# Masks and relative bias of attention: added by VectorE in PSUM, fused with the row maximum, in place of matmuls

## The chip, the cores and the metric

The kernel runs on one core of one Trainium2 chip. The metric is the device time of one execution in microseconds. Before the change it is 3609.16 us in the median of three runs (3609.14 to 3613.13).

## What is computed

A sequence of T = 512 tokens of width 1024 goes through two blocks of two layers each. The first block mixes with RWKV-7 heads beside four causal attention heads ("MOBA"; at this length plain causal attention) in layer 0 and with dilated attention in layer 1. The second block mixes, in both of its layers, with differential attention, retention and a short convolution, gated. MLPs follow each mixer. What matters here are the three kinds of attention:

```python
# MOBA: 4 heads of width 128, causal
p = softmax(q @ k.T * 128**-0.5  where key <= query)

# dilated: 8 heads; three query groups share keys and values; one softmax over all three
#   group q0: keys at distance 0..128; q1: every 4th key; q2: every 16th key (all causal)
wts = softmax(stack(lses));  o = sum(wts[g] * outs[g])

# differential: 4 heads, two maps of width 64 each, bias by distance from a table of 32 buckets
s = einsum('bhmqd,bhmkd->bhmqk', qb, kh) + bias[None, :, None]
s = where(dist >= 0, s, neg)
p = softmax(s);  a = p[:, :, 0] - lam * p[:, :, 1];  o = a @ v
```

## The kernel before

**Layout.** Activations lie transposed: channels on the 128 partitions (P), the 512 tokens (T) in the free dimension, as tiles of 128x512 f32. All weights stream from HBM in units of up to 128x1024 through a ring of three slots. ScalarE copies a unit to its high half (`split_hi`, L326), VectorE subtracts to get the low half (`split_lo`, L334), and TensorE does three matmuls of 512 columns for each 128x128 tile (`product`, L352 to L354). The halves are made three units ahead.

**Order of work.** A stage is a list of (work, tick) pairs; `run` walks the same list once for each engine, so each engine issues its instructions in that order and waits on semaphores. `behind` puts followers between the ticks of a lead. In the attention stages the lead is `project` (one weight unit for each tick, 8x3 matmuls, then for most tiles a rope on VectorE, L584 to L588), and attention follows with one unit for each tick. Stages end with all engines meeting; each stage begins with what SyncE (SP) is given in `loads`, and then SP refills the weight ring.

**Attention.** `attention` (L767) does one unit for each head and each block i of 128 queries; i runs over 0 to 3, so MOBA has 16 units, the dilated stage 32, and each differential layer 16. G is the number of score maps of a unit: 1, 3 and 2. In a tick u TensorE transposes the probabilities of the unit before (L812), computes for each map the scores of unit u against (i+1) key blocks (L822, f32, which the hardware takes as two passes; the dilated group q0 only against the last two blocks), and then adds masks and biases: for each key block one more matmul into the same PSUM region (L824). A mask is `ident` times a 128x128 bf16 mask tile (`k.m`), a bias is a 128x128 f32 piece of a Toeplitz tile times `flip`, the matrix that reverses the order. Then it multiplies the values with the probabilities of the unit before (L833) once ScalarE has copied the transposed probabilities (L847) and VectorE has copied the output of the unit two before (L866).

VectorE waits for all scores and adds of the unit, takes the maximum of each map (L873), then either scales both (L876, differential) or takes the maximum over the maps and scales it (L879, L880). ScalarE does exp with the row sum (L854). VectorE combines the maps and normalises (L884 to L888 or L893 to L896).

**Adds by stage.** MOBA has one mask for each unit (16). A dilated head has 27 (two maps with i+1 blocks and one with at most 2, over i = 0 to 3), eight heads 216. A differential head has 20 biases and 8 masks; four heads and two layers make 160 biases and 64 masks.

**Bias by distance.** In `prologue` (L452) TensorE and ScalarE make a row of 640 values for each of the four heads, on four partitions. SP stores it to DRAM (`bias_dram`, L475), waits for the store (L476) and for the loads (L477), and then the stage ends. At the head of each differential stage `load_bias` reads four Toeplitz tiles of 128x512 from it. `head_norms` prepares queries and keys of that stage; its GpSimd part zeroes four half tiles.

Of the kernel before, what the change touches and what calls it, by code (L numbers as in the profile page):

```python
# [72 lines left out]
SECOND = [("cos2", T), ("sin2", T), ("decay", 4 * T), ("mean128", P), ("flip", P)]  # L73
CONST_PARTS = [layout(part) for part in (COMMON, FIRST, SECOND)]
CONSTS, CONST_W = layout(COMMON + FIRST + SECOND)
MASKS = ["ident", "causal", "band", "four", "fourcausal", "sixteen", "sixteencausal"]
# [3 lines left out]
def constants():  # L80
    c = np.zeros((P, CONST_W), np.float32)

    def put(name, value):
        at, width = CONSTS[name]
        c[:, at:at + width] = value
# [28 lines left out]
    put("flip", a + b == P - 1)  # L114
# [11 lines left out]
    masks = {"ident": (d == 0) * 1.0, "causal": np.where(d >= 0, 0, NEG), "band": np.where(d <= 0, 0, NEG),  # L126
             "four": np.where(d % 4 == 0, 0, NEG), "fourcausal": np.where((d % 4 == 0) & (d >= 0), 0, NEG),
             "sixteen": np.where(d % 16 == 0, 0, NEG), "sixteencausal": np.where((d % 16 == 0) & (d >= 0), 0, NEG)}
    m = np.concatenate([masks[k] for k in MASKS], 1).astype(np.float32)

    dist = np.maximum(np.arange(T + P) - (P - 1), 0)
# [74 lines left out]
class Core:  # L206


    def __init__(self, nc, ctx, wts):
# [8 lines left out]
        self.mask = ctx.enter_context(nc.sbuf_tensor("mask", [P, len(MASKS) * P], BF16))  # L218
# [49 lines left out]

    def m(self, name):
        n = MASKS.index(name)  # L270
        return self.mask[:, n * P:(n + 1) * P]
# [180 lines left out]
def prologue(k, stack, first_const, x_in, const_in, mask_in, vec_in, onehot_in, relb_in, bias_dram):  # L452
# [8 lines left out]
    masks = k.tile(4, 2)[:, 0:len(MASKS) * P]  # L461
    with nc.Block() as block:
        @block.sync
        def _(sp):
            sp.dma_start(k.xT[:, :, :], x_in).then_inc(loaded, 16)
            sp.dma_start(k.vec[:, :], vec_in).then_inc(loaded, 16)
            sp.dma_start(masks, mask_in).then_inc(loaded, 16)
# [7 lines left out]
            sp.dma_start(bias_dram, row).then_inc(stored, 16)  # L475
# [291 lines left out]
def attention(k, heads, scale, prob, probT, banks, ready=None, difference=None):  # L767
# [11 lines left out]
    scores_done, maxima, exps_done, probs_ready, turned, turned_copied, out_done, out_copied, chain = \  # L779
# [12 lines left out]
    def tensor(pe, u):  # L792
# [22 lines left out]
        if u < U:  # L815
# [1473 lines left out]
```

## Time and profile before

| | |
|---|---|
| median of 3 runs | 3609.16 us |
| the profiled execution (its span) | 3613.4 us |
| TensorE busy | 3361.5 us, 93% |
| TensorE weight loads | 2642.1 us, 73% |
| VectorE busy | 1894.1 us, 52% |
| ScalarE busy | 1181.1 us, 33% |
| mean granted TensorE clock | 0.963 of full speed |
| HBM read | 258.69 MB |

Durations and spans below come from the one profiled execution; it is 4.2 us longer than the median of the runs. TensorE records overlap, since matmuls are pipelined: what one costs in a full stream is the distance from its start to the next one's, not its record. A record "x3" of the timeline is three instructions of the same kind in a row, from the first's start to the last's end. A time in brackets behind a row is the idle time of the engine before it, with what ended it.

### The profile page before, as it was taken

What the parts mean: (1) busy time and instruction counts of PE and PEld (TensorE: products, weight loads), DVE (VectorE), ACT (ScalarE), POOL (GpSimd) and SP (SyncE); (2) the same over time, 40 slices, a digit from 0 to 9 for tenths busy, and PEclk for the clock granted to TensorE, in tenths of its full rate; (3) what the DMA queues carried; (4) which work ended last, traced back from release to release, by engine and by line L of the source; (5) the groups of instructions that cost most, each with busy time, mean ns of one, the idle gap of its engine ahead of it and who ended that gap; (6) DMA issues with size and microseconds to landing.
All of it is one profiled execution on the core that took longest, in us unless ns stands there. A gap on an engine that the chain in (4) does not pass through costs nothing. (4 is left out here: it accounts for less than half of the span.)

```text
span 3613.4 us, 38618 instructions
## 1 busy us (share of the span) xinstructions
PE 3361.5 (93%) x15320; PEld 2642.1 (73%) x15320; DVE 1894.1 (52%) x2791; ACT 1181.1 (33%) x1849; POOL 185.8 (5%) x165
## 2 busy tenths in 40 slices
PE   7978897999989998899989999999999999999999
PEld 5658785788857775688857758778887766878887
DVE  3673444524267774434256674464646656456463
ACT  3332222423233332423244232342334323233232
POOL 0123220000000000000000000000000000000000
PEclk9989898999999998999999999999999989999999
DMA  4110001222211111222221112222222111222222
GB/s 155 60 57 1 1 1 47 70 95 96 100 52 66 59 60 57 70 93 94 93 79 59 65 41 94 99 86 89 97 89 90 59 47 58 93 86 92 97 88 75
DMA packets 38587, 263.28 MB, mean 73 GB/s; under 512 B 4324, under 2 KB 4708, under 8 KB 10632
## 3 DMA queue, kind: packets, MB, share of 16 engines
q1 hardware_dynamic: 38408, 260.82, 21.2%
q8 instruction: 122, 2.00, 0.2%
q14 instruction: 57, 0.47, 0.0%
HBM read 258.69 MB, written 2.11 MB: 72 GB/s over the span
## 5 line engine op out<-in xcount | busy, mean ns | idle before, releaser
L352 PE MATMUL psum<-space,w_hi 128*128 128x512 f32 x3672 | 1475.3, 402 | 61.8 <-DVE space L510 27.4
L353 PE MATMUL psum<-space,w_hi 128*128 128x512 f32 x3672 | 1457.9, 397 | 0.0
L354 PE MATMUL psum<-space,w_lo 128*128 128x512 f32 x3672 | 1456.9, 397 | 0.0
L334 DVE TENSOR_TENSOR w_lo<-ring,w_hi 128x1024 fp32r<-128x1024 f32 (+1 forms) x495 | 587.3, 1187 | 714.1 <-ACT w_hi L326 714.1
L352 PEld LDWEIGHTS psum<-space,w_hi 128*128 128x128 f32 x3672 | 697.0, 190 | 242.1 <-issue 67.0
L354 PEld LDWEIGHTS psum<-space,w_lo 128*128 128x128 f32 x3672 | 696.8, 190 | 164.9
L353 PEld LDWEIGHTS psum<-space,w_hi 128*128 128x128 f32 x3672 | 697.6, 190 | 162.7 <-issue 4.4
L326 ACT ACTIVATE w_hi<-ring 128x1024 fp32r<-128x1024 f32 (+1 forms) x495 | 506.0, 1023 | 906.3 <-PE psum L354 852.7
L854 ACT ACTIVATE space<-psum,small 128x256 f32<-128x256 f32 (+3 forms) x176 | 88.5, 509 | 241.5 <-DVE small L880 146.7
L873 DVE TENSOR_REDUCE small<-psum 128x1 f32<-128x256 f32 (+3 forms) x176 | 74.0, 465 | 129.0 <-PE psum L824 128.9
L1485 DVE TENSOR_TENSOR space<-space 128x512 f32<-128x512 f32 x64 | 44.3, 692 | 177.6 <-ACT space L1477 177.6
L822 PE MATMUL psum<-space 128*128 128x256 f32 (+3 forms) x352 | 129.0, 457 | 0.0
L1477 ACT ACTIVATE space<-psum 128x512 f32<-128x512 f32 x64 | 38.3, 598 | 223.0 <-PE psum L354 223.0
L833 PE MATMUL psum<-space 128*128 128x128 f32 x400 | 68.5, 306 | 42.7 <-DVE space L866 39.4
L847 ACT ACTIVATE space<-psum 128x128 f32<-128x128 f32 (+1 forms) x80 | 34.9, 437 | 184.0 <-PE psum L812 184.0
L833 PEld LDWEIGHTS psum<-space 128*128 128x128 f32 x400 | 55.7, 207 | 53.6 <-issue 47.1
L1850 DVE TENSOR_TENSOR psum<-psum,space 128x512 f32<-128x512 f32 x48 | 33.6, 699 | 106.6 <-PE psum L354 106.5
L654 DVE SCALAR_TENSOR_TENSOR xT<-xT,psum 128x512 f32<-128x512 f32 x96 | 65.3, 680 | 8.9 <-PE psum L354 8.9
L664 POOL TENSOR_TENSOR space<-space 128x512 f32<-128x512 f32 x18 | 23.2, 1291 | 858.8 <-ACT space L640 858.8
L1518 ACT ACTIVATE space<-psum,vec 128x512 f32<-128x512 f32 x44 | 34.3, 779 | 100.6 <-DVE psum L1531 100.6
L812 PE MATMUL psum<-constants,space 128*128 128x128 f32 x200 | 38.1, 291 | 28.8 <-DVE space L896 16.4
L1525 ACT ACTIVATE space<-space 128x512 fp32r<-128x512 f32 x44 | 27.9, 633 | 113.0 <-DVE space L1546 113.0
(257 smaller groups left out, 3110.9 us busy)
## 6 DMA issues: line engine op xcount, KB each, us to landing
ring<-in_weights SPq DMA_DIRECT2D x212, 1024.0 KB, 4.8
ring<-in_weights SPq DMA_DIRECT2D x28, 704.0 KB, 4.0
ring<-in_weights SPq DMA_DIRECT2D x4, 896.0 KB, 4.4
ring<-in_weights SPq DMA_DIRECT2D x3, 832.0 KB, 4.4
xT<-in_x SPq DMA_DIRECT2D x1, 2048.0 KB, 7.6
space<-bias_by_distance SPq DMA_DIRECT2D x8, 256.0 KB, 3.8
out<-xT SPq DMA_DIRECT2D x1, 2048.0 KB, 6.3
constants<-in_const SPq DMA_DIRECT2D x1, 1664.0 KB, 6.8
```

The costliest lines, as they stand in the source:

```text
L326: act.activation(self.w_hi[:, n % AHEAD, 0:UNITS[n] * P], self.raw(n), ACT.Copy).then_inc(self.hi_ready, 1)
L334: dve.tensor_tensor(self.w_lo[:, n % AHEAD, w], self.raw(n), self.w_hi[:, n % AHEAD, w].bitcast(F32), ALU.subtract).then_inc(self.lo_ready, 1)
L352: pe.matmul(out, hi, rhs.hi(first + at), start=(at == 0), stop=False)
L353: pe.matmul(out, hi, rhs.lo(first + at), start=False, stop=False)
L354: last = pe.matmul(out, lo, rhs.hi(first + at), start=False, stop=(at == total - 1))
L654: dve.scalar_tensor_tensor(out=k.x(t), in0=k.x(t), scalar=scale, in1=k.bank(t % nb), op0=ALU.mult, op1=ALU.add).then_inc(added, 1)
L822: last = pe.matmul(s_bank[g][:, lo:hi], q[:, i * P:(i + 1) * P], key[:, lo:hi], start=True, stop=not adds)
L833: last = pe.matmul(o_bank[:, 0:P], heads[h][1][:, b], probT[:, b], start=(j == 0), stop=(j == i))
L854: act.activation(prob[g][:, lo:hi], s_bank[g][:, lo:hi], ACT.Exp, bias=nm, scale=scale, accum_out=s[:, 3 + g:4 + g]).then_inc(exps_done, 1)
L873: ch(dve.reduce_max(s[:, g:g + 1], s_bank[g][:, first(i):(i + 1) * P], AX_X))
L1477: act.activation(buf[t % 2], k.bank(t % 8), ACT.Relu).then_inc(relu_done, 1)
L1485: dve.tensor_tensor(buf[t % 2], buf[t % 2], buf[t % 2], ALU.mult).then_inc(squared, 1)
```

## The change

1. In `attention`, TensorE does only the score matmuls, and each one signals for itself. VectorE replaces each maximum by one `tensor_tensor_reduce` over the scores in PSUM, in place: out = (scores + bias) x (-scale), and the minimum along the row into `s[:, g]`. Where one maximum over the maps is wanted (MOBA, dilated), the minimum of the map before is the start value of the next, so they wait for one another. The pairwise maxima and the scaling are gone. ScalarE's exp takes scale -1 and that minimum as its bias, and waits for it. VectorE's wait for the transposes (`turned`) moves behind these reductions.
2. Masks are whole rows instead of tiles: a bf16 tile of 128x512 for MOBA; for the dilated stage 128x1280 f32, a new load on SP at the head of the stage (640 KB), which VectorE waits for once. The mask load of the prologue shrinks from 128x896 to 128x512.
3. The biases: `bias_dram` now has 4 x 128 rows of 640 values. The prologue writes each head's row 128 times, by a DMA whose source is the four partitions with a step of zero. The four Toeplitz tiles are read as 128 rows of 512 values, each row one element on, so that no flip is needed; `flip` leaves the constants. GpSimd adds the causal mask to the last 128 columns of each tile in `head_norms`, and VectorE waits for it once a head. TensorE no longer waits for the bias load.

```diff
-            sp.dma_start(masks, mask_in).then_inc(loaded, 16)
+            sp.dma_start(masks, mask_in[:, 0:T]).then_inc(loaded, 16)
...
             sp.wait_ge(bias_copied, 2)
-            sp.dma_start(bias_dram, row).then_inc(stored, 16)
+            sp.dma_start(bias_dram, row.unsqueeze(1).to_broadcast([4, P, T + P])).then_inc(stored, 16)
             sp.wait_ge(stored, 16)
...
-            for g, (q, key, first, terms) in enumerate(heads[h][0]):
+            for g, (q, key, first, bias) in enumerate(heads[h][0]):
                 lo, hi = first(i), (i + 1) * P
-                adds = [(j, a) for j in range(lo // P, i + 1) for a in terms(i, j)]
-                last = pe.matmul(s_bank[g][:, lo:hi], q[:, i * P:(i + 1) * P], key[:, lo:hi], start=True, stop=not adds)
-                for n, (j, (lhsT, rhs)) in enumerate(adds):
-                    last = pe.matmul(s_bank[g][:, j * P:(j + 1) * P], lhsT, rhs, start=False, stop=(n == len(adds) - 1))
-            last.then_inc(scores_done, 1)
+                pe.matmul(s_bank[g][:, lo:hi], q[:, i * P:(i + 1) * P], key[:, lo:hi], start=True,
+                          stop=True).then_inc(scores_done, 1)
...
-            act.wait_ge(maxima, u + 1)
...
-                nm = s[:, 6 + g:7 + g] if difference is not None else s[:, 6:7]
-                act.activation(prob[g][:, lo:hi], s_bank[g][:, lo:hi], ACT.Exp, bias=nm, scale=scale,
+                top = g if difference is not None else G - 1
+                act.wait_ge(lowest, G * u + top + 1)
+                act.activation(prob[g][:, lo:hi], s_bank[g][:, lo:hi], ACT.Exp, bias=s[:, top:top + 1], scale=-1.0,
...
-            dve.wait_ge(scores_done, u + 1)
+            if i == 0 and bias_ready is not None:
+                bias_ready(dve, h)
+            for g, (q, key, first, bias) in enumerate(heads[h][0]):
+                scores = s_bank[g][:, first(i):(i + 1) * P]
+                end = bias.shape[-1]
+                dve.wait_ge(scores_done, G * u + g + 1)
+                if difference is None and g >= 1:
+                    dve.wait_ge(lowest, G * u + g)
+                dve.tensor_tensor_reduce(out=scores, in0=scores, in1=bias[:, end - ((i + 1) * P - first(i)):end], scale=-scale,
+                                         scalar=s[:, g - 1:g] if difference is None and g >= 1 else 3.0e38, op0=ALU.add,
+                                         op1=ALU.min, accum_out=s[:, g:g + 1]).then_inc(lowest, 1)
             if u >= 1:
                 dve.wait_ge(turned, fills(u) + (units[u][1] == 0) + 1)
-            for g, (q, key, first, terms) in enumerate(heads[h][0]):
-                ch(dve.reduce_max(s[:, g:g + 1], s_bank[g][:, first(i):(i + 1) * P], AX_X))
-            ch.sync()
-            if difference is not None:
-                dve.tensor_scalar(s[:, 6:8], s[:, 0:2], -scale, None, ALU.mult).then_inc(maxima, 1)
-            else:
-                for g in range(1, G):
-                    ch.then(dve.tensor_tensor(s[:, 0:1], s[:, 0:1], s[:, g:g + 1], ALU.max))
-                dve.tensor_scalar(s[:, 6:7], s[:, 0:1], -scale, None, ALU.mult).then_inc(maxima, 1)
...
+            pool.wait_ge(loaded, 80)
+            for h in range(4):
+                own = k.tile(30 + h)[:, T - P:T]
+                pool.tensor_tensor(own, own, k.mask[:, T - P:T], ALU.add).then_inc(masked, 1)
...
+                def load_masks(sp):
+                    sp.dma_start(dilated_masks[:, :], mask_in[:, T:T + DILATED_W]).then_inc(masks_loaded, 16)
...
-                            with nc.allow_non_contiguous_dma(reason="one Toeplitz tile per row shift"):
-                                for head in range(4):
-                                    toeplitz = bass.AP(bias_dram.tensor, head * (T + P), [[1, P], [P, TB], [1, P]])
-                                    sp.dma_start(blocks(k.tile(30 + head)), toeplitz).then_inc(bias_loaded, 16)
+                            for head in range(4):
+                                toeplitz = bass.AP(bias_dram.tensor, head * P * (T + P) + P, [[T + P - 1, P], [1, T]])
+                                sp.dma_start(k.tile(30 + head), toeplitz).then_inc(bias_loaded, 16)
...
-    bias_dram = nc.dram_tensor("bias_by_distance", (4, T + P), F32, kind="Internal").ap()
+    bias_dram = nc.dram_tensor("bias_by_distance", (4, P, T + P), F32, kind="Internal").ap()
```

## Rows read from the trace of the kernel before

**Rows 1.** The page: busy time of each engine, share of the span, instructions.
```profile
PE 3361.5 (93%) x15320; PEld 2642.1 (73%) x15320; DVE 1894.1 (52%) x2791; ACT 1181.1 (33%) x1849; POOL 185.8 (5%) x165
```
**Rows 2.** Stretches: start:end, length, busy by engine, clock, DMA share, GB/s.
```profile
1060.00:1340.00 280.00, 268.82 (x1364) 210.96 (x1363) 201.86 (x484) 105.99 (x261) 0.00 (x0) 1.00 0.19 64
1340.00:1395.00 55.00, 37.51 (x170) 26.83 (x170) 30.02 (x87) 19.09 (x51) 0.00 (x0) 0.75 0.06 20
1890.00:2050.00 160.00, 150.77 (x769) 121.31 (x769) 109.44 (x189) 61.05 (x112) 0.00 (x0) 1.00 0.17 60
```
**Rows 3.** TensorE's waits, total, times, longest: dilated stage, its tail, differential layer 0.
```profile
PE psum L833 <- DVE space L866: 6.4, 13, 1.3
...
PE psum L812 <- DVE space L896: 12.2, 4, 5.1
...
PE psum L833 <- DVE space L866: 6.7, 4, 2.2
```
**Rows 4.** Groups by line and form, the adds: count, busy us, mean ns.
```profile
L824 PE MATMUL psum<-mask 128*128 128x128 bf16 x296 | 46.8, 226 | 0.0
L824 PE MATMUL psum<-constants,space 128*128 128x128 f32 x320 | 46.1, 275 | 0.0
```
**Rows 5.** Timeline of TensorE, a differential unit with i=1: start, us, what.
```profile
2044.28 0.60 PE L822 MATMUL psum<-space 128*128 128x256 f32 x2
2044.71 0.61 PE L824 MATMUL psum<-constants,space 128*128 128x128 f32 x4
2045.16 0.22 PE L824 MATMUL psum<-mask 128*128 128x128 bf16 x1
2045.21 0.65 PE L822 MATMUL psum<-space 128*128 128x256 f32 x2
```
**Rows 6.** Groups by line and form, VectorE: count, busy us, mean ns.
```profile
L1850 DVE TENSOR_TENSOR psum<-psum,space 128x512 f32<-128x512 f32 x48 | 33.6, 699 | 106.6 <-PE psum L354 106.5
...
L873 DVE TENSOR_REDUCE small<-psum 128x1 f32<-128x512 f32 x36 | 23.4, 686 | 45.9 <-PE psum L824 45.9
...
L879 DVE TENSOR_TENSOR small<-small 128x1 f32<-128x1 f32 x64 | 10.2, 159 | 2.2
...
L880 DVE TENSOR_SCALAR small<-small 128x1 f32<-128x1 f32 x48 | 7.4, 154 | 1.7
...
L1055 DVE TENSOR_TENSOR_SCAN space<-constants,space 128x512 f32<-128x512 f32 x4 | 5.7, 1427 | 0.0
```
**Rows 7.** Timeline of ScalarE between two exps of a dilated unit.
```profile
1170.90 0.19 ACT L854 ACTIVATION_READ_ACCUMULATOR space<-psum,small 128x1 f32 x1
1170.99 0.57 ACT L854 ACTIVATE space<-psum,small 128x384 f32<-128x384 f32 x1
```
**Rows 8.** Timeline of VectorE in the unit of rows 5.
```profile
2045.45 0.28 DVE L866 COPY space<-psum 128x128 f32<-128x128 f32 x1
```
**Rows 9.** Timeline in the dilated tail, unit with i=1: first scores, last scaling.
```profile
1359.80 1.06 PE L822 MATMUL psum<-space 128*128 128x256 f32 x2
...
1364.97 0.15 DVE L880 TENSOR_SCALAR small<-small 128x1 f32<-128x1 f32 x1
```
**Rows 10.** Stretches of the prologue, columns as in rows 2 (last: GB/s).
```profile
4.00:20.00 16.00, 2.29 (x4) 0.33 (x4) 0.00 (x0) 3.69 (x5) 0.00 (x0) 1.00 1.01 409
...
21.00:22.00 1.00, 0.00 (x0) 0.00 (x0) 0.00 (x0) 0.00 (x0) 0.00 (x0) 1.00 0.37 154
```
**Rows 11.** Timeline of the prologue: bias store, last preparation, next stage's first load.
```profile
14.43 0.32 SPq L475 DMA_DIRECT2D bias_by_distance<-space  x1
...
23.45 3.49 DVE L334 TENSOR_TENSOR w_lo<-ring,w_hi 128x1024 fp32r<-128x1024 f32 x3
27.23 0.34 SPq L1939 DMA_DIRECT2D space<-in_lora  x1
```
**Rows 12.** Timeline of SP: the Toeplitz loads of differential layer 0.
```profile
1846.21 3.34 SPq L2085 DMA_DIRECT2D space<-bias_by_distance  x4
```
**Rows 13.** The adds of line 824: ns min/median/max, first and last start.
```profile
L824 PE MATMUL psum<-constants,space x320: 272/275/275, 1893.7 to 2941.2; 128*128 128x128 f32 x160
```

More of the change, by code:

```diff
@@ L113, in constants @@
     put("sum64", block)
-    put("flip", a + b == P - 1)
     put("pair", block)
@@ L125, in constants @@
     d = a - b
[L126 to L131, printed above, removed]
+    causal, band, none = np.where(d >= 0, 0, NEG), np.where(d <= 0, 0, NEG), np.zeros((P, P))
+    four, sixteen = np.where(d % 4 == 0, 0, NEG), np.where(d % 16 == 0, 0, NEG)
+    masks = {"near": [band, causal], "four": [four] * 3 + [np.minimum(four, causal)],
+             "sixteen": [sixteen] * 3 + [np.minimum(sixteen, causal)]}
+    m = np.concatenate([none] * 3 + [causal] + [b for k in DILATED for b in masks[k]], 1).astype(np.float32)
+    dist = np.maximum(T - np.arange(T + P), 0)
     nf = np.maximum(dist, 1).astype(np.float32)
@@ L460, in prologue @@
     row = k.tile(2, 2)[0:4, 0:T + P]
-    masks = k.tile(4, 2)[:, 0:len(MASKS) * P]
+    masks = k.tile(4)
     with nc.Block() as block:
@@ L764, in rms_norm, with attention @@
     return w
-def attention(k, heads, scale, prob, probT, banks, ready=None, difference=None):
-    scores_done, maxima, exps_done, probs_ready, turned, turned_copied, out_done, out_copied, chain = \
+def attention(k, heads, scale, prob, probT, banks, ready=None, difference=None, bias_ready=None):
+    scores_done, lowest, exps_done, probs_ready, turned, turned_copied, out_done, out_copied, chain = \
         (k.sem() for _ in range(9))
@@ L1557, in head_norms @@
 def head_norms(k, l, copied, loaded, lam_v, lam_p, sq, bank):
-    squared, mean_done, root, inverse, cleared, normed, lam_sum, lam_exp, chain = (k.sem() for _ in range(9))
+    squared, mean_done, root, inverse, cleared, masked, normed, lam_sum, lam_exp, chain = (k.sem() for _ in range(10))
     src = [k.tile(4 * (n % 2) + n // 2) for n in range(8)]
@@ L1956, in head_ready @@
                     pe.wait_ge(proj.copied, v_at[h] + 1)
-                moba = attention(k, [([(k.tile(12 + h), keys[h], lambda i: 0, causal)], values[h], k.tile(12 + h))
+                moba = attention(k, [([(k.tile(12 + h), keys[h], lambda i: 0, k.mask)], values[h], k.tile(12 + h))
                                      for h in range(4)], P ** -0.5, [k.tile(37)], k.tile(38), (5, 6, 7), ready=head_ready)
@@ L2021, in head_ready, with masks_ready @@
                     pe.wait_ge(proj.copied, 5 * h + 5)
+                dilated_masks = inner.enter_context(nc.sbuf_tensor("dilated_masks", [P, DILATED_W], F32))
+                masks_loaded = k.sem()
+                near, four, sixteen = (dilated_masks[:, at:at + width] for at, width in DILATED.values())
+                def load_masks(sp):
+                    sp.dma_start(dilated_masks[:, :], mask_in[:, T:T + DILATED_W]).then_inc(masks_loaded, 16)
+                def masks_ready(dve, h):
+                    if h == 0:
+                        dve.wait_ge(masks_loaded, 16)
                 heads = []
@@ L2047, in program @@
                 schedule = schedule[:-6] + [e for t in range(6) for e in [last[t]] + fill[t]] + rest[7:]
-                run(k, schedule + ticks(down))
+                run(k, schedule + ticks(down), load_masks)
         n = feed_forward(1, n)
```

34 lines of the change are left out of this document (12 added, 22 removed).

## The prediction

> **What bounds the kernel now.** I read the page's busy times first: TensorE 93%, VectorE 52% [rows 1]. Weight products dominate, and in them one matmul follows another without a gap, so a matmul that is taken out is worth its distance to the next start. Whether that holds in the three attention stages, the only ones the change enters, I took from their stretches: in the dilated one TensorE is busy 268.8 of 280 us with VectorE at 201.9, in the differential one 150.8 of 160 with VectorE at 109.4; the dilated tail is different, 37.5 of 55 us at a clock of 0.75 [rows 2]. Then the waits of TensorE: nearly all are L833, the product with the values, waiting for L866, VectorE's copy of the output before: 6.4 us in 13 waits in the dilated stage, 6.7 in 4 in a differential one; in the tail it is L812 waiting for the probabilities, 12.2 us [rows 3]. So TensorE sets the pace, with VectorE close behind in some ticks and ahead of it in the tails.
>
> **Adds removed from TensorE.** There are 296 masks in bf16 and 160 biases in f32 (two records each, 320) [rows 4]. Their price is start to start, not the 226 and 275 ns of the records, which overlap: four f32 records go from 2044.71 to 2045.16, 0.111 us each; one bf16 record from 2045.16 to 2045.21, 0.055 us [rows 5]. MOBA: 16 x 0.055 = 0.9 us. Dilated: 216 x 0.055 = 11.9. Differential, both layers: 320 x 0.111 + 64 x 0.055 = 39.0, that is 19.5 a layer. Together 51.8 us, if nothing else ends last.
>
> **What VectorE does in their place.** Each maximum (686 ns for 512 columns) becomes one fused instruction that also reads the mask, writes PSUM and stores the minimum. No row shows it. The nearest without the reduction is an addition with PSUM in and out, 699 ns for 512 columns; the nearest running reduction of two inputs is the scan, 1427 ns, twice that [rows 6]. An accumulator's own price shows only on ScalarE: behind an exp stands a read of 0.19 us, and the next exp starts 0.09 us after it [rows 7]. I take the addition plus 0.1 us, since stream and operands are those of the addition; the ends are plus 0 and plus 0.75 for 512 columns. Beside it, two pairwise maxima of 159 and a scaling of 154 ns go per dilated unit [rows 6] (with gaps 0.57 us), against 3 x 0.1 and two links between dependent instructions at about 0.12: VectorE's series stays as long as it was. What is won is its start: the first fused instruction needs only the first scores, not all scores and adds.
>
> A rule bears on that 0.1. The trace shows ScalarE's accumulate as two records. The Trainium skill, page "VectorE: DVE Perf Modes", section "Two Vector instructions with no wait between them", says that a Vector instruction that writes out its accumulator is two instructions, the main one and an accumulator read; no row here shows it on VectorE, and it would turn plus 0 into something like the value taken.
>
> **Differential stage, per layer 15.4 us.** Of 19.5 us, the adds in the four ticks where L833 waits for L866 (two at i=0, two at i=2; 2 x 0.55 + 2 x 1.45 = 4.0) are hidden by that wait. VectorE's chain before them starts earlier and gives back 1.8. Two more ticks turn into waits: in the one shown, L866 starts at 2045.45 and takes 0.28, and without adds the scores would be done at 2045.2, so L833 goes at about 2045.8 instead of 2045.2 [rows 5, 8]; with its like 1.9 us is lost. 19.5 - 4.0 + 1.8 - 1.9 = 15.4; two layers 30.8.
>
> **Dilated stage, 10 + 6 us.** Per head 27 adds, 1.5 us. At i=0 nothing waits: 0.2. At i=1 the adds and the wait of 0.15 go: 0.5. At i=2 and 3 VectorE's series (rope, copy, reductions) is the limit; its earlier start is worth about 0.4 and 0.3. That is 1.4 for each of 7 heads, 10 us. In the tail each unit's whole chain is exposed: at i=1 scores start at 1359.80 and the last scaling ends at 1365.12, 5.3 us [rows 9]; without adds (0.6 at half clock) and with only one reduction left behind the last scores, about 3.7. The four units give 1.2, 1.6, 1.9 and, since other work already fills the last, 1.2: 6 us. The load of 640 KB of masks is queued on SP ahead of weight loads; the ring holds three slots and no TensorE wait of this stage names a DMA, so I cost it at nothing, 2 us if that cover were gone.
>
> **MOBA 2 us.** 0.9 of adds and 16 scalings, partly behind VectorE's RWKV work.
>
> **The new waits.** VectorE waits for the masks (head 0) and for GpSimd's additions to the bias; behind it in its queue stand the rope and the halving of weights (L334), which TensorE needs. Both waits are over long before: the bias is loaded from 1846.21 on, the additions are four instructions behind that, and the first biased scores come at 1893.7 [rows 12, 13]; the masks are issued at the head of their stage, whose layer norm and six projections run first. The longer rows of the new Toeplitz loads and the shorter constants are covered too: nothing. A fused instruction of one unit waits for the one before it; that is in the links above. ScalarE waits for them as it did for the scaling.
> **Sum of gains.** It is 2 + 16 + 30.8 = 48.8 us; with the fused instruction at its ends, 20 to 58.
>
> **The prologue pays.** The bias store was 10 KB from 4 partitions; now each row is written 128 times: 4 x 128 x 2560 B = 1.31 MB. It is issued at 14.43 behind the loads, which keep all 16 engines at 409 GB/s until about 21.4 (154 GB/s in the last microsecond), SP waits for it, and the next stage starts on all engines only at the block's end, 27.23 now [rows 10, 11]. Nothing covers it: VectorE's last preparation ends at 26.9 [rows 11]. One engine moves 409/16 = 25.6 GB/s. The smaller mask saves 0.5 us of loading, so the store begins at 20.9; from its last byte to the start of the stage I count 1.1 us. Bounds: spread over 16 engines 3.2 us, hidden, and the stage starts 0.5 earlier; four engines, one for each source row, 12.8 us, end 33.7, start 34.8 (+7.6); one stream at a time, since all the bytes come out of the same four partitions, 51.3 us, end 72.2, start 73.3 (+46.1). The nearest row is the 10 KB store itself, which shows no rate. I take the last: the source is four adjacent partitions read 128 times, and no load in this trace reaches its rate other than from many partitions.
>
> A rule speaks here against the change. The Trainium skill, page "SBUF — State Buffer", section "Door 1: The DMA port swizzle", says that transfer rate depends on how many of 16 ports the partitions reach, and that partitions 0 to 3 share one, 27.6 GB/s for 1 MiB. By that the store takes an estimated 47.5 us and the kernel comes out near 3603; no run here shows it yet. If four engines each kept the rate of the rows, the time would be the first rival's.
>
> **Sum.** Against the profiled execution: 3613.4 - 48.8 + 46.1 = 3610.7 us. The median of the runs, 3609.2, lies 4.2 us under that span, so I forecast 3606.5.
>
> **Rivals.**
> 1. The store runs on four engines in parallel (or is spread wider): 3609.2 - 48.8 + 7.6 = 3568.0, and 3559.9 if hidden. For it: transfers here are spread over engines, at 25.6 GB/s each. Against: one small source.
> 2. Slower: the serial store, and a fused instruction at the price of the scan. VectorE's work grows by about 5.4 us of reductions per dilated head (12 of them, doubled) against 2.3 of small steps removed, and its ticks there become longer, not shorter; the gain shrinks to 20 us and the time is 3609.2 - 20 + 46.1 = 3635. It decides from about 0.25 us more than the addition for each fused instruction, as each 0.1 us costs some 6.5 us (21 of 28 dilated ticks, the tail, 6 ticks a layer); then the sum passes 3616.
> 3. The adds are free, because VectorE hides all of them, though the store costs: 3655. Against it: 93% busy TensorE and only 4 waits a layer; small.
>
> **How the numbers follow.** About 0.2% (7.2 us) is what a measurement of this kernel can tell from no change. Forecast case 0.52, of which 0.12 below 3602 (the gain at 54 or more, or the store at 43), 0.33 within, 0.07 above. Rival 1: 0.31, all faster. Rival 2: 0.14, slower by most of it (0.13). Rival 3: 0.03, slower. So faster 0.43, same 0.34, slower 0.23. The range must reach rival 1, whose chance is over 0.2, and half of rival 2: 3563 to 3622. The likeliest case's own range is 3597 to 3618.
>
> **What would show it.** In the profile after: the first loads of the next stage near 73 us instead of 27.2 (35 if four engines); no L824; the fused line at 0.39, 0.52, 0.65 and 0.79 us for 128 to 512 columns, and whether a second record follows; differential stage and layer 15 us shorter each, with six waits on L866; the dilated tail 6 us shorter. The prediction is wrong if the store is fast, or if the fused instruction is far from 0.8 us.

## The result, and the profile after

The kernel after takes 3624.28 us in the median of 7 runs (3619.15 to 3635.18), the kernel before 3609.14 (3605.82 to 3613.13): a ratio of 1.0039, 95% interval 1.0028 to 1.0050. It is 15 us slower, where 3606.5 was predicted and the range ended at 3622.

The profiled execution of after has a span of 3621.0 us against 3613.4, both at a mean granted clock of 0.963. The page of after, busy time by engine:

```profile
PE 3308.2 (91%) x14704; PEld 2590.3 (72%) x14704; DVE 1893.8 (52%) x2823; ACT 1182.1 (33%) x1849; POOL 188.6 (5%) x173
```

Beside [rows 1]: TensorE lost 616 instructions and 53.3 us of work, VectorE has the same 1894 us. So the change did what it says, and the span grew all the same. To see where, I took the start of the same weight product in both traces, at the borders of the stages, and subtracted:

| stretch | after minus before at its end, us | gain of the stretch | predicted |
|---|---|---|---|
| prologue | +43.5 | -43.5 | -46.1 |
| MOBA and the rest of layer 0 | +42.9 | 0.6 | 2 |
| dilated, seven heads | +43.8 | **-0.9** | **10** |
| dilated tail | +38.2 | 5.6 | 6 |
| differential layer 0 (starts at +39.2) | +26.0 | 13.2 | 15.4 |
| differential layer 1 (starts at +25.7) | +9.2 | 16.5 | 15.4 |
| last MLP, end | +7.6 | 1.6 | 0 |

Where the code is the same in both, the offset still moves by 1 to 2 us for a stretch, so a term of that size can't be read from one pair of traces. One stretch moves far more: the retention and the short convolution behind the attention of differential layer 0 are the same code in all twelve traces of this case and take 50.6 to 64.9 us. That matters for the comparisons below.

**The prologue.** SP's timeline of after, the store and the next stage's first load, then three stretches (start:end, length, busy by engine, clock, DMA share, GB/s):

```profile
13.16 0.79 SPq L472 DMA_DIRECT2D bias_by_distance<-space  x1
...
70.70 0.34 SPq L1938 DMA_DIRECT2D space<-in_lora  x1
```
```profile
30.00:60.00 30.00, 0.00 (x0) 0.00 (x0) 0.00 (x0) 0.00 (x0) 0.00 (x0) 1.00 0.23 26
1106.00:1386.00 280.00, 257.88 (x1183) 201.06 (x1182) 204.20 (x489) 106.25 (x262) 0.00 (x0) 0.99 0.19 64
1386.00:1436.00 50.00, 33.45 (x136) 24.77 (x135) 28.88 (x83) 17.25 (x48) 0.00 (x0) 0.83 0.06 22
```

For 30 us no engine does anything, and the DMA engines move 26 GB/s where the loads of [rows 10] reach 409. The load that stood at 27.23 in [rows 11] stands at 70.70. The share of 0.23 is worth reading: it is 3.7 of 16 engines, as many as there are source rows, and each moves 26/3.7 = 7 GB/s where in the loads each moves 25. The packets of the store agree: three or four are under way at any moment, and a packet of 2560 bytes takes 373 ns, against 102 ns when it is fast. Four engines run in parallel and share what one alone would reach.

The second of these rows stands against the first of [rows 2]: in 280 us of the dilated stage TensorE has 11 us less to do, VectorE 2.3 us more, and the stretch holds no more heads than before. The third is the tail.

**TensorE's waits** in the dilated stage, in its tail, and in differential layer 0 (total, times, longest):

```profile
PE psum L827 <- DVE space L860: 15.4, 11, 2.1
...
PE psum L809 <- DVE space L891: 9.9, 3, 4.8
...
PE psum L827 <- DVE space L860: 9.7, 6, 3.5
```

L827 is the product with the values, L860 the output copy (L833 and L866 before). Against [rows 3]: 6.4 us in 13 waits became 15.4 in 11. The adds of seven heads had cost 10.4 us, and 9.0 of it came back as waiting for the same instruction.

**The fused instruction** by form (count, busy us, mean ns, idle before):

```profile
L871 DVE DVE_READ_ACCUMULATOR2_ANT small<- 128x1 f32 x176 | 24.9, 141 | 0.0
...
L871 DVE CUSTOM_DVE_ANT_0 psum<-psum,space 128x512 f32<-128x512 f32 x16 | 11.2, 700 | 22.9 <-PE psum L818 22.1
...
L871 DVE CUSTOM_DVE_ANT_0 psum<-psum,dilated_masks,small 128x512 f32<-128x512 f32 x8 | 6.1, 758 | 1.7 <-PE psum L818 0.6
...
L871 DVE CUSTOM_DVE_ANT_0 psum<-psum,dilated_masks 128x384 f32<-128x384 f32 x8 | 4.5, 567 | 0.9 <-PE psum L818 0.7
...
L871 DVE CUSTOM_DVE_ANT_0 psum<-psum,dilated_masks 128x128 f32<-128x128 f32 x8 | 2.4, 300 | 11.6 <-PE psum L818 11.6
```

700 ns for 512 columns is the addition of [rows 6] to a nanosecond: adding the minimum to it costs nothing in the stream. Behind each one stands a second record, the read of the accumulator, 141 ns. A start value taken from a tile instead of a constant adds 58 to 61 ns (758 against 700).

### The profile page after: what moved, and what is told of

Read it like the earlier page. It is cut to its first block and busy times, and to the rows that moved or that the text cites. A ratio compares the mean times of both kernels' runs of the same rounds, so it can differ in the third digit from the quotient of the medians.

```text
span 3621.0 us, 37498 instructions
## 1 busy us (share of the span) xinstructions
PE 3308.2 (91%) x14704; PEld 2590.3 (72%) x14704; DVE 1893.8 (52%) x2823; ACT 1182.1 (33%) x1849; POOL 188.6 (5%) x173
## 5 line engine op out<-in xcount | busy, mean ns | idle before, releaser
L827 PE MATMUL psum<-space 128*128 128x128 f32 x400 | 68.4, 307 | 62.2 <-DVE space L860 58.3
L827 PEld LDWEIGHTS psum<-space 128*128 128x128 f32 x400 | 58.2, 209 | 88.5 <-issue 74.4
L818 PE MATMUL psum<-space 128*128 128x256 f32 (+3 forms) x352 | 108.2, 436 | 0.0
L818 PEld LDWEIGHTS psum<-space 128*128 128x128 f32 x352 | 59.8, 200 | 22.8 <-issue 14.4
```

The lines of the kernel that those rows point to most:

```text
L827: last = pe.matmul(o_bank[:, 0:P], heads[h][1][:, b], probT[:, b], start=(j == 0), stop=(j == i))
```

## The experiments

### The store: how many partitions, or how many engines?

Theory A: its rate depends on the partitions that it reads. Theory B: on the number of engines that its form allows, four. Three kernels write the same 1.31 MB from 16, 64 and 128 partitions. In the first two the matmuls make each head's row on 4 or 16 partitions by a widened left operand; in the third, eight matmuls and eight copies put all four rows on every partition, and nothing is repeated by the source.

```diff
-    row = k.tile(2, 2)[0:4, 0:T + P]
+    row = k.tile(2, 2)[0:16, 0:T + P]
...
-            sp.dma_start(bias_dram, row.unsqueeze(1).to_broadcast([4, P, T + P])).then_inc(stored, 16)
+            sp.dma_start(bias_dram.rearrange("h (r c) t -> (h r) c t", r=4), row.unsqueeze(1).to_broadcast([16, P // 4, T + P])).then_inc(stored, 16)
```
```diff
-            sp.dma_start(bias_dram, row.unsqueeze(1).to_broadcast([4, P, T + P])).then_inc(stored, 16)
+            sp.dma_start(bias_dram.rearrange("h p t -> p h t"), rows).then_inc(stored, 16)
```

> The changed kernel, with the bias row of each head on four partitions (16 in all, side by side) in place of one; the same 1.31 MB and 512 packets of 2560 B go to DRAM, each source partition read 32 times. In the changed kernel the store moved 26 GB/s with 0.23 of the 16 engines busy, and the next stage's first load came at 70.7 us. Theory A (the rate goes by how many groups of partitions the source reaches; four adjacent partitions are one group of some 26 GB/s): four groups, about 105 GB/s, 12.5 us, first load of the next stage at 35 us, the kernel about 36 us faster than the changed one. Rival B (the number of engines limits; 16 of them carry it now): 3.2 us at 409 GB/s, hidden, first load at 26.5 us. Rival C (reading with a step of zero is slow whatever the place): near 70 us as before.

> As src16, with each head's row on 16 partitions, so that the source is partitions 0 to 63 and each is read 8 times. Theory A as the Trainium skill puts it (page SBUF — State Buffer, section Door 1: partitions 0 to 63 reach only 8 of the 16 ports): about 200 GB/s while the store runs, 6.4 us. If each source row has a rate of its own (26/4 = 6.5 GB/s in the changed kernel), 64 rows reach the 16 engines' 409 GB/s and the store takes 3.2 us. The next stage would start at 27 to 28.5 us with the first and at 26.5 with the second.

> The changed kernel with its rows made on all 128 partitions: TensorE multiplies each head's column, repeated 128 times, with the one-hot table (8 matmuls in place of 2), ScalarE copies 8 pieces, and one store of 128 partitions x 4 rows writes the same 1.31 MB. Theory: the prologue's 43.5 us are the store's alone. The store then runs at about 400 GB/s in 3.3 us behind the loads, the next stage starts at 26 to 28 us, and the kernel is 43 us faster than the changed one: 28 to 36 us faster than before, 3573 to 3581. Rival: the bytes themselves or the additional matmuls cost, and the next stage starts after 35 us.

Stretches in which the store runs by itself: 16 partitions, 64 (three microseconds in a row), 128:

```profile
26.00:30.00 4.00, 0.00 (x0) 0.00 (x0) 0.00 (x0) 0.00 (x0) 0.00 (x0) 1.00 0.93 102
```
```profile
22.00:23.00 1.00, 0.00 (x0) 0.00 (x0) 1.00 (x3) 0.00 (x0) 0.00 (x0) 1.00 1.07 412
23.00:24.00 1.00, 0.00 (x0) 0.00 (x0) 1.00 (x2) 0.00 (x0) 0.00 (x0) 1.00 1.00 236
24.00:25.00 1.00, 0.00 (x0) 0.00 (x0) 1.00 (x2) 0.00 (x0) 0.00 (x0) 1.00 0.59 146
```
```profile
22.00:24.00 2.00, 0.00 (x0) 0.00 (x0) 1.65 (x4) 1.34 (x2) 0.00 (x0) 1.00 1.03 413
```

With 16 partitions all 16 engines are at work (0.93) and still move 102 GB/s, 7 each, as the four did. So the number of engines doesn't set the rate; the source does: 26 GB/s from partitions 0 to 3, four times that from 0 to 15. This run alone can't tell whether each source row has a rate of its own (6.5 GB/s) or each group of four adjacent rows shares one, since both give about 104.

The 64 rows speak for a shared rate, but not all the way. At first they move 412 GB/s; then, with every engine still at work (share 1.00), 236, where rows with a rate of their own would have stayed at the loads' 409; the 146 are the end, with engines already done (0.59). A packet takes 102 ns in the first part and 193 in the second, between the 373 ns of 4 and 16 rows and the 102 of 128 rows. With 128 partitions the store runs at 413.

The Trainium skill, page "SBUF — State Buffer", section "Door 1: The DMA port swizzle", has partitions 0 to 3 on one port, 0 to 15 on four and 0 to 63 on eight, with 27.6, 104 and 196 GB/s measured for 1 MiB. The first two runs agree, with 26 and 102 GB/s; the third doesn't settle at 196.

The next stage starts at 32.36, 26.12 and 26.57 us, where 35 was expected by theory A for 16 partitions, and 27 to 28.5 or 26.5 for 64. The last two starts don't tell 64 partitions from 128, since the store ends at 25.2 and 25.1 us. One run each gave 3580.81 us (16) and 3575.07 (64); 128 partitions gave 3573.61 (3571.54 to 3577.35), ratio 0.9891 [0.9874, 0.9907] to the before of its session. The time from after's 3624.28 to this is 51 us, of which 70.70 - 26.57 = 44.1 are the store's; the traces, 49.4 us apart, have the rest spread thinly over the later stretches. So the new attention by itself makes the kernel 1.1% faster, and the store takes more than that away.

### The adds alone: what does TensorE get for them?

The kernel before with every add left out (no causal masks, no biases), and nothing else changed: VectorE keeps its maxima and scalings.

```diff
-                adds = [(j, a) for j in range(lo // P, i + 1) for a in terms(i, j)]
+                adds = []
```

> The kernel before with all 456 masks and biases left out of the computation and nothing put in their place; maxima and scalings as before. It shows what TensorE's part of the change is worth by itself. Theory A (VectorE hides the adds in the dilated steady state): the period of a dilated head falls from 42.1 us by no more than 0.9, since VectorE only starts a little earlier; the dilated tail shrinks by about 2.5 us, a differential layer by 16, the whole by 36 to 42 us. Rival B (TensorE bound all through): 51.8 us in all, of which 1.5 per dilated head.

It takes 3589.24 us (3586.09 to 3591.64), ratio 0.9945 [0.9928, 0.9961]: 23 us under the before of its session, where 36 to 42 were expected and the adds' distances sum to 51.8. The offsets against before give 2.5 us of it in the seven dilated heads, 4.1 in the tail, 5.9 and 5.2 in the two differential layers, where 16 each were expected. Its waits over the whole kernel say where a part of the rest is:

```profile
PE psum L833 <- DVE space L866: 60.5, 36, 7.2
```

The kernel before has 39.4 us in 27 waits there, so 21 us of the adds' time came back as waiting for VectorE's copy. Another part is TensorE's clock. In the third head of differential layer 0 TensorE waits for the copy, and from the end of that wait on its granted clock is 0.51, the lower of its two levels (1.2 and 2.4 GHz); the next stretch is back at 0.99. The timeline row of the wait, then the two stretches (columns as in [rows 2]):

```profile
1998.34 1.20 PE L833 MATMUL psum<-space 128*128 128x128 f32 x4 [2.39 <-DVE space L866]
```
```profile
1998.30:2001.70 3.40, 3.36 (x10) 2.91 (x11) 2.00 (x7) 2.18 (x5) 0.00 (x0) 0.51 0.00 0
2001.70:2006.30 4.60, 4.60 (x22) 3.72 (x22) 2.26 (x4) 0.00 (x0) 0.00 (x0) 0.99 0.00 0
```

Weight products start 0.43 us apart in the first stretch and 0.23 in the second, so time at the lower level is nearly half lost. Counting it gives this account of a differential layer against before, in us. The column of the clock is an estimate: the additional time at the lower level, times (0.43 - 0.23)/0.43.

| kernel, layer | gain by the offsets | more waiting for the copy | lost by the clock (estimate) | sum |
|---|---|---|---|---|
| no adds, layer 0 | 5.9 | 6.2 | 6.3 (13.6 more at the lower level) | 18.4 |
| no adds, layer 1 | 5.2 | 6.3 | 7.9 (17.0 more) | 19.4 |
| after, layer 0 | 13.2 | 3.0 | 3.2 (6.8 more) | 19.4 |
| after, layer 1 | 16.5 | 3.1 | 0 | 19.6 |

The adds of a layer are worth 19.5 by the prediction's distances, and each row comes near that. So the price of an add holds, and what isn't gained went into waits and into the slower clock behind them.

The length of the ticks, from one unit's first scores to the next one's, for a dilated head (i = 0 to 3):

| kernel | i=0 | i=1 | i=2 | i=3 | head |
|---|---|---|---|---|---|
| before | 7.57 | 8.03 | 9.53 | 16.92 | 42.05 |
| no adds | 7.53 | 7.80 | 9.31 | 16.93 | 41.57 |
| after | 7.53 | 7.58 | 9.68 | 17.35 | 42.14 |

At i=1 the exchange gives 0.45 us, as predicted; at i=2 and 3 it loses 0.15 and 0.43, and there even adds that cost nothing would have given 0.2 and 0.0.

### The chain between the fused instructions

Theory A: in those ticks VectorE's own series, copy, reductions, exp, is the path, and the fused instructions made it longer, because each waits for the one before. VectorE's timeline of the unit i=2, before and after:

```profile
1168.28 0.28 DVE L866 COPY space<-psum 128x128 f32<-128x128 f32 x1
1168.48 1.33 DVE L873 TENSOR_REDUCE small<-psum 128x1 f32<-128x384 f32 x3
1169.85 0.35 DVE L879 TENSOR_TENSOR small<-small 128x1 f32<-128x1 f32 x2
1170.23 0.15 DVE L880 TENSOR_SCALAR small<-small 128x1 f32<-128x1 f32 x1
```
```profile
1211.86 0.28 DVE L860 COPY space<-psum 128x128 f32<-128x128 f32 x1
1212.17 0.57 DVE L871 CUSTOM_DVE_ANT_0 psum<-psum,dilated_masks 128x384 f32<-128x384 f32 x1
1212.65 0.14 DVE L871 DVE_READ_ACCUMULATOR2_ANT small<- 128x1 f32 x1
1212.94 0.63 DVE L871 CUSTOM_DVE_ANT_0 psum<-psum,dilated_masks,small 128x384 f32<-128x384 f32 x1
1213.48 0.14 DVE L871 DVE_READ_ACCUMULATOR2_ANT small<- 128x1 f32 x1
1213.77 0.49 DVE L871 CUSTOM_DVE_ANT_0 psum<-psum,dilated_masks,small 128x256 f32<-128x256 f32 x1
1214.18 0.14 DVE L871 DVE_READ_ACCUMULATOR2_ANT small<- 128x1 f32 x1
```

From the end of the copy to the value that the exp needs: 1168.56 to 1170.38 is 1.82 us before, 1212.14 to 1214.32 is 2.18 after. The series was predicted to stay as long as it was.

The test takes the chain away: all three start from a constant and none waits for another (so the exp's bias is only the last map's minimum, and the common minimum over the maps is left out; all three exps still share one bias, which cancels when they are divided by their sum, so what is missing is only the guard against larger values in the first two maps). It ran on the kernel after, and again with the rows on 128 partitions.

```diff
-                if difference is None and g >= 1:
-                    dve.wait_ge(lowest, G * u + g)
...
-                                         scalar=s[:, g - 1:g] if difference is None and g >= 1 else 3.0e38, op0=ALU.add,
+                                         scalar=3.0e38, op0=ALU.add,
```

> The changed kernel with one thing left out: in the dilated stage each fused instruction starts from a constant in place of the minimum of the map before, and so does not wait for it; the exps then use the last map's own minimum, so the softmax over the three maps is left out in part. Theory A (the dilated steady state gained nothing because VectorE's series between the copy of the output and the last minimum became longer, by the accumulator's record of 141 ns and about 0.14 us of waiting behind it for each link): without two links per unit, 0.4 us less for each of the ticks at i=1 to 3, and the period of a head falls from 42.1 to 41 us, 8 us in all. Rival B (TensorE sets the pace there and the adds were never on its path for another reason): the period stays at 42.1.

> The kernel with the bias rows on all 128 partitions, and in the dilated stage no chain between the three maps: each fused instruction starts from 3.0e38 and doesn't wait for the one before it, so only the last map's minimum serves as the exp's bias (the minimum over the three maps is left out). Theory A, the chain of dependent fused instructions sets the dilated tick: a head takes about 40.3 us instead of 42.1, 8 heads give 10 to 14 us against the 3573.6 of the same kernel with the chain, so 3560 to 3564. Theory B, the 10 us of the single look were the clock of that execution: the head stays at 42.1 and the time at 3571 to 3577.

The same unit in the second of these kernels:

```profile
1161.56 0.28 DVE L863 COPY space<-psum 128x128 f32<-128x128 f32 x1
1161.86 0.57 DVE L872 CUSTOM_DVE_ANT_0 psum<-psum,dilated_masks 128x384 f32<-128x384 f32 x1
1162.35 0.14 DVE L872 DVE_READ_ACCUMULATOR2_ANT small<- 128x1 f32 x1
1162.35 0.60 DVE L872 CUSTOM_DVE_ANT_0 psum<-psum,dilated_masks 128x384 f32<-128x384 f32 x1
1162.86 0.14 DVE L872 DVE_READ_ACCUMULATOR2_ANT small<- 128x1 f32 x1
1162.86 0.47 DVE L872 CUSTOM_DVE_ANT_0 psum<-psum,dilated_masks 128x256 f32<-128x256 f32 x1
1163.24 0.14 DVE L872 DVE_READ_ACCUMULATOR2_ANT small<- 128x1 f32 x1
```

Without the chain the next fused instruction starts together with the read of the one before, 0.49 and 0.51 us after its start; in the chain it is 0.77 and 0.83. A link costs 0.28 to 0.32 us: the overlap with the read is lost, 0.14 us pass behind the read, and the start value comes from a tile. The series is 1.54 us instead of 2.18, and TensorE follows. The first scores of two heads in a row, in after and in this kernel:

```profile
1193.92 0.83 PE L818 MATMUL psum<-space 128*128 128x128 f32 x6
...
1236.05 0.83 PE L818 MATMUL psum<-space 128*128 128x128 f32 x6
```
```profile
1144.87 0.83 PE L821 MATMUL psum<-space 128*128 128x128 f32 x6
...
1185.12 0.83 PE L821 MATMUL psum<-space 128*128 128x128 f32 x6
```

42.13 us became 40.25; the ticks are 7.53, 7.31, 8.71 and 16.70. In the first of the two kernels the head is 40.29, and the offset against before falls by 10.4 us over the seven heads. Yet its one time, 3622.64 us, is only 1.6 below after's median, so by the time alone it decides nothing. The traces show where the gain went: into the stretch behind the attention of differential layer 0, the same code in after (first row) and here:

```profile
2091.75:2143.76 52.01, 42.59 (x124) 18.91 (x122) 33.53 (x46) 16.16 (x26) 5.03 (x4) 0.85 0.06 22
2072.03:2136.91 64.88, 55.46 (x123) 22.12 (x122) 34.17 (x46) 16.17 (x26) 5.02 (x4) 0.66 0.05 18
```

It took 12.9 us longer, at a granted clock of 0.66 instead of 0.85. The second kernel gives 3563.21 us (3562.14 to 3570.68), ratio 0.9854 [0.9832, 0.9877], beside 0.9891 [0.9874, 0.9907] with the chain: the intervals touch, and the profiled spans are 10.2 us apart, 13 of it in the dilated stage and its tail. The length of the head leaves no room for theory B, a matter of clock: both traces agree on it, against 42.1 in after, and no head compared here has a granted clock under 1.00.

### The copy that TensorE waits for

The named wait is on the output copy. It needs little (0.28 us), but stands in VectorE's queue behind ropes, halvings and reductions. ScalarE is 33% busy [rows 1].

```diff
+        if 2 <= u <= U + 1:
+            h, i = units[u - 2]
+            act.wait_ge(out_done, u - 1)
+            act.activation(heads[h][2][:, i * P:(i + 1) * P], o_bank[:, 0:P], ACT.Copy).then_inc(out_copied, 1)
...
-        if 2 <= u <= U + 1:
-            h, i = units[u - 2]
-            dve.wait_ge(out_done, u - 1)
-            dve.tensor_copy(heads[h][2][:, i * P:(i + 1) * P], o_bank[:, 0:P]).then_inc(out_copied, 1)
```

> The changed kernel with the copy of the finished output (VectorE, 281 ns, 80 times) done by ScalarE at the head of its tick. TensorE waits 58.3 us for that copy, which stands in VectorE's queue behind rope and halving. Theory A (the wait is only the copy's place in the queue): most of the 58.3 us goes, at least 30 us, 8 in the dilated steady state (the period of a head falls to 41 us or less). Rival B (VectorE's whole series is the limit, so the wait moves to the probabilities, L809 in the changed kernel, which waits 14.7 us now): under 10 us.

> The kernel before with the copy of the output on ScalarE and nothing else. TensorE waits 39.4 us for that copy. Theory A: 20 to 35 us faster than before. Rival B (the wait moves to the probabilities): under 8 us.

> Both: rows on 128 partitions and the copy of the output on ScalarE. If the adds were only hidden by VectorE's late copy, they come out now: at least 45 us faster than before_out_on_act's own gain would leave it, since 51.8 us of adds are gone from a TensorE that no longer waits; that is 3530 to 3545. Rival B (VectorE's series still last in the dilated stage): the gain over before_out_on_act stays at 30 to 38 us.

On after it gives 3569.79 us (one run), 54 under after's median, and the wait on VectorE's copy is gone; the wait for the probabilities grew from 14.7 to 27.6 us. On before it gives 3576.55 (3568.02 to 3584.87), ratio 0.9907 [0.9885, 0.9929]. With the rows on 128 partitions and the copy on ScalarE: 3525.67 (3524.1 to 3533.36), ratio 0.9770 [0.9753, 0.9788]; 3530 to 3545 were expected.

The last two ran in one session and differ by the change of this case with its store mended: 50.9 us by the medians. The profiled executions are 41.8 apart. By the offsets it is 3.5 us in MOBA and the rest of layer 0, 8.8 in the dilated stage and its tail, and 18.7 in each differential layer. In the two stretches behind the differential attention, the same code, 9.7 of it is lost again: 56.9 against 52.1 us at clocks of 0.75 and 0.85, then 48.7 against 43.8 at 0.82 and 0.91.

The heads are the cleaner measure. In a differential layer TensorE waits for no output copy in either kernel, the clock is 1.00 in both, and three heads shrink by 14.6 us, 4.87 each, where a head's adds are worth 4.88. So there the price of the adds was right, and what kept TensorE from getting it was VectorE's late copy, with the slower clock behind the waits. In the dilated stage a head shrinks only from 40.73 to 39.9 us, 0.8 where its adds are worth 1.5, and at i=2 the tick grows from 8.80 to 9.30: the chain still holds TensorE there, which now waits 7.9 us for the probabilities instead of 0.3.

A last kernel puts both findings together and computes all of the reference: three independent minima, one wait, one reduction of the three values.

```diff
+            if G == 3:
+                dve.wait_ge(lowest, G * (u + 1))
+                dve.tensor_reduce(s[:, 6:7], s[:, 0:3], AX_X, ALU.min).then_inc(least, 1)
```

> The kernel with the rows on 128 partitions and the output copy on ScalarE, and the chain between the three maps replaced: three independent minima, one wait, and one reduction of the three values (128x3) that gives the exp's bias. It computes all of the reference. Theory A, VectorE's series still holds up TensorE there (39.93 us a head): two waits between fused instructions and two start values read by pointer go (about 0.4 us a unit), one small reduction and one wait come (0.15 + 0.14), so 0.1 us a unit, 3 us in 32 units: 3521 to 3524. Rival, with the copy gone VectorE has slack in the tick, TensorE sets it at 39.9: no change, 3524 to 3527, except in the tail.

It takes 3513.48 us (3500.24 to 3515.49), ratio 0.9703 [0.9671, 0.9735]: the fastest here, 3% under before, and apart from the 0.9770 of the version with the chain. The wait behind the last read and the small reduction:

```profile
1152.49 0.14 DVE L876 DVE_READ_ACCUMULATOR2_ANT small<- 128x1 f32 x1
1152.66 0.16 DVE L881 TENSOR_REDUCE small<-small 128x1 f32<-128x3 f32 x1
```

From the first fused instruction (1151.11) to the value is 1.71 us, against 2.15 with the chain in after; a head takes 38.8 us against 39.9, and its tick at i=2 8.08 against 9.30. I had expected 3 us for the whole kernel, with links at 0.2 each; at 0.3, and 1.1 us in each head, it is about 9 in the dilated stage by the offsets. The other 5 us between the profiled executions, 13.8 apart, aren't this edit's: the two stretches behind the differential attention are 9.8 shorter at a higher clock (0.85 and 0.93 against 0.75 and 0.82), and the RWKV part of layer 0 is 4.4 longer.

## Why the prediction was wrong

**What bounds the kernel.** The prediction said "TensorE sets the pace, with VectorE close behind in some ticks", and later that at i=2 and 3 of the dilated stage VectorE's series is the limit. The second was right and wasn't followed through: if VectorE is the limit, a matmul less on TensorE gives nothing there. 268.8 busy of 280 us [rows 2] hid how much that was, since busy TensorE time included adds done while VectorE was late; 13 waits of 6.4 us [rows 3] were what the adds had left visible.

**Price of the adds.** Right in the differential layers: 4.88 us a head against 4.87, once no copy of VectorE's stands before TensorE. That the whole comes out at 50.9 us beside 51.8 shows less, since that difference holds VectorE's changed work too, and no run takes the adds alone away from a kernel with the copy on ScalarE.

**Dilated stage, 10 us predicted, -0.9 found.** This is the step that failed. Of the 1.4 us for a head, 0.7 was for an earlier start of VectorE's series at i=2 and 3. But there the reductions start when rope and copy are through, not when the scores are: the copy ends 2.9 us after the first scores, and the scores without adds are done at 1.5 to 2. Removing adds for nothing gives 0.2 at i=2 and 0.0 at i=3. The other term is "links between dependent instructions at about 0.12", measured 0.28 to 0.32. In the unit shown: three fused instructions cost 0.19 more than three maxima (1.52 against 1.33; predicted 0.3), two links 0.63 (predicted 0.24), small instructions removed 0.57 (as predicted), and the copy no longer overlaps the first of them, 0.11 (not thought of). That is +0.36 where "VectorE's series stays as long as it was" has 0. Less the 0.2 that the missing adds give at i=2, it is the 0.15 by which that tick grew.

**Dilated tail, 6 us.** 5.6: right in size. The kernel without adds gains 4.1 of it. The granted clock there rose too, from 0.75 [rows 2] to 0.83, and no run separates its share.

**Differential layers, 30.8 us.** 13.2 + 16.5 = 29.7 (and 14.8 + 16.5 with the store mended), with the six waits on the copy that were predicted. The waiting grew by 3.0 and 3.1 us a layer, where the prediction's terms (-4.0 + 1.8 - 1.9) had 4.1. What they lacked is the clock, some 3 us in layer 0 by the account above. So the mechanism was right here; the waits were put 1 us too high and the clock at nothing.

A third head takes 43.30 us before, 41.67 without adds, 39.26 after. The 2.4 us between the last two are not all VectorE's shorter path to the exp. They lie in the tick i=2 alone (11.85 and 9.45 us), where the wait for the copy is 2.4 us without adds and 1.6 after; that is 0.8. The rest is about what the 3.4 us at a clock of 0.51 cost behind the longer wait. The unit with i=2 shows the shorter path, before and after:

```profile
2010.48 1.01 DVE L873 TENSOR_REDUCE small<-psum 128x1 f32<-128x384 f32 x2
2011.53 0.17 DVE L876 TENSOR_SCALAR small<-small 128x2 f32<-128x2 f32 x1
2011.74 0.58 ACT L854 ACTIVATE space<-psum,small 128x384 f32<-128x384 f32 x1 [4.22 <-DVE small L876]
```
```profile
2042.19 0.57 DVE L871 CUSTOM_DVE_ANT_0 psum<-psum,space 128x384 f32<-128x384 f32 x1
2042.67 0.60 DVE L871 CUSTOM_DVE_ANT_0 psum<-psum,space 128x384 f32<-128x384 f32 x1
...
2042.85 0.58 ACT L848 ACTIVATE space<-psum,small 128x384 f32<-128x384 f32 x1 [2.99 <-DVE small L871]
```

Before, the first exp starts 1.26 us after the first maximum: it waits for both maxima and the scaling. After, it starts 0.66 us after the first fused instruction, beside the second. Two maps with a minimum each have no chain, so here the fused instructions shorten the series that they lengthen in the dilated stage.

**MOBA, 2 us.** 0.6, below what a pair of traces can tell.

**Prologue, +46.1.** +43.5. The value was taken as "one stream at a time"; what the trace shows is four engines that share 26 GB/s. Same price, other picture: rival 1 had the number of engines right, and was wrong that each keeps its 25.6 GB/s. That the rate of one engine in the loads (25.6) and the rate of this source (26) are so near each other is luck. By the Trainium skill, page "SBUF — State Buffer", section "Door 1: The DMA port swizzle", the store was to take an estimated 47.5 us; its first packet starts at 20.6 us and its last ends at 69.9, 49.4 us at 26 GB/s for 1.31 MB.

**The fused instruction.** The accumulator's second record was announced by the Trainium skill, page "VectorE: DVE Perf Modes", section "Two Vector instructions with no wait between them"; the trace agrees, 141 ns. Where nothing depends on it, the next instruction starts beside it, and it costs only some 0.06 us. What it makes dear is a dependent next instruction. Rival 2 was wrong in its mechanism (700 ns, not 1427) and right about the place: VectorE's ticks in the dilated stage got longer. It came from the links.

**From one execution to the median.** The steps sum to 3610.7 for an execution like the profiled one; that took 3621.0, 10.3 more, nearly all of it the dilated term. The other 7.5 us of the miss are the conversion: the profiled execution of before had a span 4.2 us over the median, and I carried that over; after's lay 3.3 us under its own. In that a span was compared with a median of times, and every run here has a time 1.7 to 2.1 us longer than its span: after's profiled run has a span of 3621.0 and a time of 3622.74, only 1.5 under its median. Either error alone would have left the time inside the range; the two together took it out. The seven runs of after go from 3619 us at a mean granted clock of 0.965 to 3635 at 0.959. A span's distance from the median belongs to that execution, not to the kernel, and the range should have had some 5 us for it on each side.

## What to carry to other kernels

Taking work from the busiest engine pays only in those ticks in which nothing else is late; a wait that stays the last one there, here a small copy in a crowded queue, should be moved first. A gain behind such a wait is small twice over: part of it turns into waiting, and behind the longer wait TensorE's clock can fall, as in the kernel without adds. A fused reduction is cheap when its results are independent and dear as a chain, so reduce separately and combine once. A store that repeats a source must start from many partitions, and a stage that waits for it at a full meeting pays for all of it.

## What the runs showed of the hardware that I had not expected

- A store from four adjacent partitions moves 26 GB/s with four engines at work, one from 16 partitions 102 with sixteen; each engine moves 7 GB/s in both.
- From partitions 0 to 63 it moved 412 GB/s in one microsecond and 236 in the next, with all engines at work in both. The Trainium skill, page "SBUF — State Buffer", section "Door 1: The DMA port swizzle", has these partitions on 8 of 16 ports and 196 GB/s measured for 1 MiB; both rates are above that. Why the first part is so fast isn't settled here.
- Behind a wait of TensorE of 2.39 us its granted clock was 0.51 for 3.4 us, with weight products 0.43 us apart instead of 0.23. The same code behind the attention of differential layer 0 took 52.0 us at a clock of 0.85 and 64.9 at 0.66. What decides between the two isn't shown.
- `tensor_tensor_reduce` with both large operands in PSUM and a mask in SBUF streams like a plain addition (700 ns for 512 columns); its accumulator read is 141 ns, hidden unless the next instruction depends on it, which then starts 0.28 to 0.32 us later.
